# Routed bias between two loops of expert visits, and the last visit's four chunk pairs in a row

## The reference, cut to what matters

```
xn   = RMSNorm(x)                                   # 512 x 1024, float32
gate = softmax over the 4 best of 32 router logits
for each expert e, over the tokens routed to it:
    hid = xn @ w_gate_up[e] + b_gate_up[e]          # 1024 x 2048, float32: 8 MB
    act = (clip(up) + 1) * gate_ * sigmoid(1.702 * gate_)
    y   = act @ w_down[e] + b_down[e]               # 1024 x 1024: 4 MB
x   += sum over the 4 experts of gate * y
out  = RMSNorm(x)
```

## Time and profile before

| | |
|---|---|
| time, median of 3 runs | 1394.98 us (1392.49 to 1396.18) |
| span of the profiled execution | 1395.8 us; the page gives no time around the span |
| PE busy, DVE, ACT, POOL | 89%, 49%, 16%, 23% of the span |
| mean granted TensorE clock | 0.973 of full speed |
| HBM traffic | 445.02 MB read, 14.81 MB written |
| chain that ended last | PE 58%, DMA 29%, DVE 7% |

### The profile page before, as it was taken

One profiled execution on the slowest core, in us unless ns is written; L12 is line 12 of the kernel. 1 busy time (PEld: TensorE's weight loads), 2 busy tenths in 40 slices (PEclk: granted clock), 3 DMA queues, 4 the chain that ended last, 5 costly groups with the idle time before them and its releaser, 6 DMA issues.

```text
span 1395.8 us, 32044 instructions
## 1 busy us (share of the span) xinstructions
PE 1241.0 (89%) x12814; PEld 585.9 (42%) x12815; DVE 679.5 (49%) x1360; ACT 223.3 (16%) x439; POOL 320.3 (23%) x432
## 2 busy tenths in 40 slices
PE   6999999999599999899899999798978887879992
PEld 3444454564235554353534445233432332335331
DVE  2898885444644364335434433345443334353428
ACT  3125543412100011000000100000110000001103
POOL 5001111000322224222223212222233222222221
PEclk9999999999799999999999999999999999999996
DMA  9212000312589999999999999999999999999996
GB/s 307 85 61 91 1 31 1 142 74 86 210 337 400 409 418 424 425 426 426 426 425 425 424 426 425 426 426 425 426 424 425 426 427 425 426 426 426 380 407 245
DMA packets 59374, 455.33 MB, mean 326 GB/s; under 512 B 13308, under 2 KB 23604, under 8 KB 34214
## 3 DMA queue, kind: packets, MB, share of 16 engines
q1 hardware_dynamic: 44262, 432.59, 74.8%
q0 software_dynamic: 11568, 18.92, 3.7%
q10 hardware_dynamic: 3504, 3.26, 0.9%
HBM read 445.02 MB, written 14.81 MB: 329 GB/s over the span
## 4 chain that ended last, share of the span: by engine, by line
PE 58%; DMA 29%; DVE 7%; issue 2%; ACT 2%; ACTq 1%; POOL 0%; SPq 0%; DVEq 0%; POOLq 0%
PE bank L2136 26%; DMA ring<-in_w_gate_up_dram 15%; PE bank L2189 14%; DMA dslots<-in_w_down_dram 14%; PE bank L1797 6%; PE bank L1987 4%; DVE dslots L1122 3%; PE bank L1792 2%; DVE hbuf L1697 1%; PE bank L1865 1%; PE bank L1872 1%; PE bank L2100 1%; PE bank L2122 1%; PE bank L1952 1%; PE bank L1956 1%
## 5 line engine op out<-in xcount | busy, mean ns | idle before, releaser
L2136 PE MATMUL bank<-ring,wq 128*32 128x512 f32 x4992 | 566.6, 601 | 64.9 <-DMA ring<-in_w_gate_up_dram 56.2
L2136 PEld LDWEIGHTS bank<-ring,wq 128*32 128x32 f32 x4992 | 208.8, 111 | 381.1 <-issue 344.3
L2189 PE MATMUL bank<-dslots,intra 128*32 128x256 f32 x5056 | 284.7, 380 | 22.6 <-DMA dslots<-in_w_down_dram 21.8
L2189 PEld LDWEIGHTS bank<-dslots,intra 128*32 128x32 f32 x5056 | 169.1, 110 | 148.3 <-issue 54.6
L1510 DVE TENSOR_REDUCE small<-bank 128x4 f32<-128x8 f32 x33 | 5.5, 166 | 409.8 <-PE bank L2100 409.8
L1007 ACT ACTIVATE zrows<-intra 128x1024 f32<-128x1024 f32 x31 | 32.8, 1059 | 790.0 <-DVE intra L1603 763.8
L1797 PE MATMUL bank<-hbuf,ring 128*128 128x512 f32 x320 | 148.5, 604 | 0.7 <-ACT hbuf L748 0.7
L616 POOL COPY idx_in<-idx 128x4 int32 (+1 forms) x32 | 11.8, 370 | 555.6 <-DVE wq L1488 534.4
L1575 DVE STREAM_TRANSPOSE wq<-bank 128x512 f32<-128x512 f32 x124 | 77.8, 685 | 71.7 <-PE bank L2136 71.7
L621 POOL DMA_INDIRECT wq<-xn_rows,idx_in x82 | 100.5, 1225 | 44.3 <-POOL idx_in L616 28.0
L626 POOL DMA_INDIRECT y_rows<-rows,idx_out x79 | 81.0, 1025 | 52.5 <-POOL idx_out L616 25.2
(11 more groups left out here) (294 smaller groups left out, 894.4 us busy)
## 6 DMA issues: line engine op xcount, KB each, us to landing
ring<-in_w_gate_up_dram SPq DMA_DIRECT2D x127, 2048.0 KB
dslots<-in_w_down_dram SPq DMA_DIRECT2D x61, 2048.0 KB
ring<-in_w_in_dram SPq DMA_DIRECT2D x12, 1024.0 KB, 13.5
ring<-in_w_out_dram SPq DMA_DIRECT2D x4, 1024.0 KB, 5.6
ring<-in_w_down_dram SPq DMA_DIRECT2D x4, 1024.0 KB
dslots<-y_rows SPq DMA_DIRECT2D x2, 2048.0 KB, 20.1
hbuf<-in_x_dram SPq DMA_DIRECT2D x4, 512.0 KB, 5.4
dslots<-in_w_down_dram SPq DMA_DIRECT2D x2, 1024.0 KB, 4.7
```

Source lines behind the costliest of these rows:

```text
L2136: ins = M(bank[g][GROUP * j:GROUP * (j + 1), :], x[:, g, c * GROUP:(c + 1) * GROUP], w[:, :, j * QD:(j + 1) * QD], start=(c == 0), stop=(c ...
L2189: ins = M(b[GROUP * j:GROUP * (j + 1), col:col + QD], actT[:, g, c * GROUP:(c + 1) * GROUP], w[:, cc, j * QD:(j + 1) * QD], start=(c == 0 ...
```

## The change

The loop of visits is cut in two at visit `MID` = 16 on PE, DVE and ACT; its body becomes a function `visit`. Between the two loops PE takes the four transposes of the gates and the four routed bias products in a row, ACT copies the gates, and DVE adds the four pieces to x2. Behind the second loop PE takes all four chunk pairs of visit 31 and then down(30). SP asks for all four chunk pairs of expert 31 and then for w_down of expert 30. DVE's `last_act` no longer waits for a down product, and writes its result to `actT_last`, a view of `qkbuf`, instead of `actT`, which down(30) still reads. On ACT the four sigmoids of the last visit stand ahead of the results of expert 30 instead of behind them.

```diff
--- before.py
+++ after.py
@@ -34,6 +34,7 @@
 GROUPS = 4
 CAP = GROUP * GROUPS
 STAGES = 4
+MID = 16
 
 
 def block_kernel(nc, x, attn_norm_w, w_in, gdn_conv_w, gdn_a_log, gdn_dt_bias, gdn_norm_w, cf_dw_w, cf_dw_b,
@@ -224,6 +225,7 @@
         u2 = view(zrows, CAP * 8, GROUPS, KC * GROUP)
         g2 = view(intra, 0, GROUPS, KC * GROUP)
         actT = view(intra, CAP * 8, GROUPS, KC * GROUP)
+        actT_last = view(qkbuf, 0, GROUPS, KC * GROUP)
         yb = view(rows, 0, GROUPS, QD)
         y_end = view(wq, CAP * 16, GROUPS, QD)
         finw = rows[:, D:2 * D]
@@ -444,12 +446,11 @@
                     down_pair(i - 1, u)
 
             for c in range(0, KC, 2):
-                if c == 4:
-                    for u in (0, 2):
-                        sp.wait_ge(d_used, m * 4 + (u + 2))
-                        down_pair(None, u)
                 sp.wait_ge(gu_used, m * KC + (c + 2))
                 gate_up(E - 1, c)
+            for u in (0, 2):
+                sp.wait_ge(d_used, m * 4 + (u + 2))
+                down_pair(None, u)
             for u in range(4):
                 sp.wait_ge(gu_used, m * KC + (KC + u + 1))
                 sp.dma_start(view(ring, u * SLOT, 2, D), down_rows(E - 1, u)).then_inc(slot_in[u], 16)
@@ -1009,19 +1010,24 @@
 
             act.sem_inc(y_ready, 1)
             sigmoid_gate(1)
-            with act.Fori(1, m + 1) as i:
+            def visit(i):
                 sigmoid_gate(i + 1)
                 act.wait_ge(d_used, i * 4 + 4)
                 act.wait_ge(landed, i * 16)
                 results((i - 1) % STAGES)
+
+            with act.Fori(1, MID) as i:
+                visit(i)
             act.wait_ge(gt_done, 1)
             A(GT, bank[7][0:E, :], ACT.Copy).then_inc(gt_copied, 1)
+            with act.Fori(MID, m + 1) as i:
+                visit(i)
+            for g in range(GROUPS):
+                act.wait_ge(g2_last, g + 1)
+                A(sg[:, g, :], g2[:, g, :], ACT.Sigmoid, scale=ALPHA).then_inc(sg_last, 1)
             act.wait_ge(d_used, m * 4 + 8)
             act.wait_ge(landed, m * 16 + 16)
             results((E - 2) % STAGES)
-            for g in range(GROUPS):
-                act.wait_ge(g2_last, g + 1)
-                A(sg[:, g, :], g2[:, g, :], ACT.Sigmoid, scale=ALPHA).then_inc(sg_last, 1)
             for g in range(GROUPS):
                 act.wait_ge(d_last, g + 1)
                 A(y_end[:, g, :], bank[g][:, 0:QD], ACT.Copy,
@@ -1619,7 +1625,7 @@
             LOOP_OWN = STEPS_IDX + STEPS_ACT
             act_part(0, 1, own.n)
             own.n += STEPS_ACT
-            with dve.Fori(1, m + 1) as i:
+            def visit(i):
                 base = (i - 1) * LOOP_OWN + own.n
                 dve.wait_ge(idx_done, i + 3)
                 dve.wait_ge(rows_known, i * 2 + 1)
@@ -1632,6 +1638,13 @@
                 hid_turn(i + 1)
                 xt_turn(i + 1)
                 act_part(i % E, i + 1, base + STEPS_IDX)
+
+            with dve.Fori(1, MID) as i:
+                visit(i)
+            for t in range(T):
+                add_bias(t)
+            with dve.Fori(MID, m + 1) as i:
+                visit(i)
 
             def last_act():
 
@@ -1672,7 +1685,7 @@
                     dve.wait_ge(sg_last, g + 1)
                     k = step(V.tensor_tensor(g2[:, g, :], g2[:, g, :], sg[:, g, :], ALU.mult))
                     after(k)
-                    V.scalar_tensor_tensor(out=actT[:, g, :], in0=u2[:, g, :], scalar=1.0, in1=g2[:, g, :],
+                    V.scalar_tensor_tensor(out=actT_last[:, g, :], in0=u2[:, g, :], scalar=1.0, in1=g2[:, g, :],
                                            op0=ALU.add, op1=ALU.mult).then_inc(act_last, 1)
 
                 turn_at = {0: turn(0)}
@@ -1682,10 +1695,7 @@
                         turn_at[g + 1] = turn(g + 1)
                     product(g)
 
-            for t in range(T):
-                add_bias(t)
             dve.wait_ge(gu_used, m * KC + 2 * KC)
-            dve.wait_ge(d_used, m * 4 + 4)
             last_act()
 
             dve.wait_ge(acc_ready, T)
@@ -2209,28 +2219,29 @@
             tokens = tokens_left(pe, 0)
             pe.wait_ge(xt_ready, 1)
             gate_up(0, first=True, known=tokens)
-            with pe.Fori(1, m + 1) as i:
+            def visit(i):
                 pe.wait_ge(xt_ready, i + 2)
                 gate_up(i)
                 pe.wait_ge(act_ready, i)
                 pe.wait_ge(y_ready, i)
                 tokens = tokens_left(pe, i - 1)
                 down(i - 1, tokens)
+
+            with pe.Fori(1, MID) as i:
+                visit(i)
+            pe.wait_ge(idx_ready, MID + 2)
+            gates_turn()
+            for t in range(T):
+                routed_bias(t)
+            pe.wait_ge(acc_ready, T)
+            with pe.Fori(MID, m + 1) as i:
+                visit(i)
             tokens = tokens_left(pe, m + 1)
             pe.wait_ge(xt_ready, m + 3)
-            pe.wait_ge(idx_ready, m + 3)
-            gates_turn()
-            gate_up(m + 1, pairs=(0,), known=tokens)
-            routed_bias(0)
-            gate_up(m + 1, pairs=(2,), known=tokens)
-            routed_bias(1)
+            gate_up(m + 1, known=tokens)
             pe.wait_ge(act_ready, m + 1)
             pe.wait_ge(y_ready, m + 1)
             down(m, tokens_left(pe, m))
-            routed_bias(2)
-            gate_up(m + 1, pairs=(4,), known=tokens)
-            routed_bias(3)
-            gate_up(m + 1, pairs=(6,), known=tokens)
 
             def last_down(u, g):
                 w = view(ring, u * SLOT, 2, D)
@@ -2238,7 +2249,7 @@
                     c = 2 * u + cc
                     for j in range(4):
                         ins = M(bank[g][GROUP * j:GROUP * (j + 1), 0:QD],
-                                actT[:, g, c * GROUP:(c + 1) * GROUP],
+                                actT_last[:, g, c * GROUP:(c + 1) * GROUP],
                                 w[:, cc, j * QD:(j + 1) * QD], start=(c == 0), stop=(c == KC - 1))
                 if u == 3:
                     ins.then_inc(d_last, 1)
```

## The result

| | before | changed |
|---|---|---|
| median | 1396.47 us (6 runs) | 1404.51 us (6 runs, 1401.48 to 1406.41) |
| ratio | | 1.0058, 95% interval 1.0048 to 1.0067 |
| span of the profiled execution | 1395.8 us | 1402.5 us |
| mean granted TensorE clock | 0.973 | 0.965 |

A run's time is some 1.8 us longer than its span (1404.32 us for the profiled execution of the changed kernel), so times are compared with times here and spans with spans.

What follows compares the result with a forecast made beforehand. The stream of weights was taken to bound the kernel. Profiled span 1395.8 us, less 2.1 in the tail, plus 3.8 at the cut, gave 1397.5, so a median of 1396.7 us; range 1390.5 to 1402.5.

Steps and rivals of the forecast that it cites:

- What bounds the kernel: Loop of visits to plane 1: the unbroken stream of weights counts, not PE; 5.17 us per unit, lateness reaches the end.
- The cover of 15.5 us: At the cut: visit 17's first chunk pair may be requested 15.5 us late at no cost, thanks to loads already asked for.
- The first bias product: At the cut: the first routed bias starts about 864.95 us, after down(14) ends about 862.5 and the gates are copied.
- The first period: At the cut: from one routed bias product to the next, 3.45 us.
- Three periods of 3.45 us and a last one of 3.31: At the cut: length of the chain of four routed bias products and additions, the last addition ending at 878.6 us.
- rival A: At the cut: bias products run at the lower clock, delay 24.4 us, stream broken by 8.9, median 1401.8; chance 0.25.
- The sequencer: At the cut: PE's branch, token count and four waits before gate_up(16) take 1.5 us, bounds 1.1 and 2.1.
- The clock on the first pair: After the cut: a lower clock adds 1.7 us to gate_up(16)'s first pair, lower bound 0.
- The tail, -2.1 us: Tail: only DVE's lateness is gained, four additions ending at 1379.85 us instead of 1381.96.
- all three just make it and land as before: Tail: planes 0, 1 and 2, though requested later, land at their old times; a 2 MB load needs 7.2 us.
- Rival C: Tail: slow loads of 1310 to 1320 us are won back, planes and end 3.0 us sooner; chance 0.11.
- 0.8 us from a span to a median: Final sum: the profiled execution taken as 0.8 us above the median of 1394.98, turning 1397.5 into 1396.7.

Runs made afterwards that it cites:

- banks_finw: Changed kernel with the four bias products in four pairs of PSUM banks and the last norm's weights requested at the cut: 1398.45 us, kernel before 1396.29.
- banks: Changed kernel with the four bias products at the cut in four different pairs of PSUM banks: 1396.9 us, kernel before 1396.5; repeated, 1400.39 against 1397.17.
- cut_only: Changed kernel with the old order of the tail, routed bias still at the cut: 1404.46 us, kernel before 1396.5.
- tail_only: Kernel before with only the new tail order (four pairs, then down(30)), bias still in the tail, no cut: 1398.6 us, kernel before 1396.5.
- banks_filled: Changed kernel with bias products in four pairs of banks, two products of no use ahead and three behind: 1396.22 us, kernel before 1397.01.
- filled: Changed kernel with products of no use, 128 rows deep, in the gaps of the bias chain at the cut: 1399.85 us, kernel before 1396.5.

## Why the prediction was wrong, step by step

- **What bounds the kernel**: right. A late load arrives at the end in full; the time behind c0(17) is 506.9 and 506.8 us.
- **The cover of 15.5 us**: right. Delay less cover and hole agree within 0.8 us in eleven of the twelve rows that have both, from 9.9 down to 0.3 and the one below nothing, which has no hole. In banks_finw they are 2.4 us apart. There the stream stood later beside PE: the last landing ahead of the cut comes 24.8 us after the end of down(14) (858.38 to 883.16), 23.6 without the norm's weights, where the kernel before has 21.4 and the other eleven 21.4 to 22.3 (reckoned alike). Its cover was 2.2 us longer by that, which is the difference. Why the stream stood later in that execution isn't known.
- **The first bias product** 2.4 us after down(14): right (2.5, from 859.27 to 861.73). **The first period** of 3.45 us: right (3.48).
- **"Three periods of 3.45 us and a last one of 3.31"**: the step that failed. The second and third period are 5.16 us, the last 5.11 (875.53 to 880.64): 5.2 us of the error. The products of the chain ran at the lower of the clock's two levels (0.50, 1.2 GHz) from the second on. The forecast had this as rival A and its price right, 1.7 us for each product, but gave it 0.25 because PE is half busy there and the clock of the earlier trace rows had fallen at 40%. One row gave a place where it fell and none where it held; the margin had nothing under it. A's own size at the cut, a break of 8.9 us, came within 0.6 us of the 9.5 measured.
- **The sequencer**: 1.5 us taken, 1.2 measured (880.64 to 881.84). **The clock on the first pair**: 1.7 taken; c0(17) is asked for 6.59 us after gate_up(16) starts in place of 4.03 (862.21 to 866.24 in the kernel before), 2.6. So the hole is 9.5 us and not 3.8.
- **The tail, -2.1 us**: the part sized is right, since from plane 2's landing to the end it is 18.5 us instead of 20.7. But "all three just make it and land as before" is wrong. Down(30) ends at 1361.6. With the weights landing 4.9 us late (1364.40 in place of 1359.45), I had it at 1359.6. Plane 0 takes 9.3 us from its request and plane 2 9.9, not the 7.2 of an empty queue: beside them stand the scatters and the load of the last norm's weights, which lands at 1377.0 between planes 0 and 1; before, it landed behind plane 2. Plane 2 comes 19.6 us after the last weights instead of 15.6. With that load early it is 17.8 us (banks_finw) instead of 19.1 (banks).
- **Rival C**: the dip of the earlier trace rows lies ahead of the end of down(29), which comes at 1324.6 us in the kernel before, 7.4 later in cut_only, 6.5 later in the changed kernel and 1.5 sooner in tail_only, so the windows are moved with it. In this order:

```profile
1310.00:1335.00 25.00, 24.91 (x306) 10.61 (x299) 13.48 (x24) 3.07 (x6) 7.73 (x10) 1.00 0.87 348
1317.00:1342.00 25.00, 23.43 (x328) 10.30 (x324) 12.54 (x24) 2.63 (x5) 7.73 (x10) 1.00 0.98 400
1316.00:1341.00 25.00, 23.56 (x313) 10.19 (x309) 12.55 (x24) 2.63 (x5) 7.73 (x10) 1.00 1.00 421
1308.00:1333.00 25.00, 25.00 (x313) 10.55 (x303) 13.85 (x27) 3.07 (x6) 7.74 (x10) 1.00 1.00 423
```

The new order removes the dip, with the cut or without it, and the cut alone makes it much shallower. The stretch from c0(17) to the last weights is 467.8 to 469.3 us in the runs at visit 16 with the new order and 470.1 to 470.5 with the old one (one run aside, which has the norm's load inside): some 1.4 us instead of C's 3.0. The forecast had the dip as free, and it was not; but the late planes use up what its removal wins. I did not find which load those 1.4 us come from.

On the two spans the account closes: 5.7 us too little at the cut and 2.2 in the tail are 7.9, and less the 2.9 by which the stream stood sooner at the cut they are the 5.0 us between the span forecast (1397.5) and the span measured (1402.5). On the medians it does not. The changed kernel is 8.0 us above before where I had 1.7, so 6.3 us are the error, and the other 1.5 of the 7.8 are the kernel before, whose median went from 1394.98 us with three runs to 1396.47 with six. That 7.9 and 7.8 look alike is luck. The forecast's 0.8 us from a span to a median mixed the two measures, but it left the 1.7 us of change as they were.

## What to carry to other kernels

Work put between two loops of a kernel that lives on its loads is free only up to a cover that can be read from the trace: landing of the next load in line, less its request, less the time of a load on an empty queue. What stands in that cover is a chain, so ask for its length at either level of the clock, and cut the handshakes out of it before moving it. And where a late product holds the buffer of the next reads, moving it last drains the queue: count what else is then asked for beside those reads.

## What the runs showed of the hardware

TensorE's granted clock fell to 0.50 in the bias chain with gaps of only 1.92 and 1.38 us (changed kernel), and also with hardly any: in banks and banks_filled the bias products (16 instructions, 32 rows deep) stood back to back, PE was busy 4.00 us in windows of 4.00, and the clock was 0.50. The longest gap ahead of them was 1.92 us in banks and 0.20 us in banks_filled. With products of 128 rows between each two of them it stayed at 1.00 (filled). So here it wasn't idle time by itself. Whether it is the 32 rows or something else in these products no run separates. The Trainium skill (TensorE: Matmul & The Clock Gate, HAM oscillation — how this bites in real kernels) ties the fall to idle gaps of PE longer than any of these. The rows of this case don't agree, and the measurement decides.

The way in which a load is late matters too. In the hole all 16 engines run dry and then land c0(17) within 0.4 us of each other, where the landings of one load were spread over 7.7 us before. The bytes that were not moved (5 MB, some 12 us at 426 GB/s) are therefore more than the 9.5 us by which the last engine, the one that counts, falls back.
